# One 32-block arena per chain, and a fourth slot in the ring of feed-forward weights

## What is computed

```python
for i in range(DEPTH):                       # DEPTH = 2
    if i == 0:  mix = gla_mixer(h, ...)      # q,k,v,r and a low-rank gate; state S_t = diag(a_t) S_{t-1} + k_t v_t^T
    else:       mix = swa_mixer(h, ...)      # 16 query heads, 4 key/value heads, window 128, sinks
    h = layer_norm(ALPHA * h + mix, ln1_g[i], ln1_b[i])
    h = layer_norm(ALPHA * h + square(relu(h @ w_up[i])) @ w_down[i], ln2_g[i], ln2_b[i])   # 1024 -> 4096 -> 1024
    gate = sigmoid(h @ ple_w_gate[i] + ple_b_gate[i])
    h = h + gate * (p[i] @ ple_w_proj[i])
```

## Time and profile before

| what | value |
|---|---|
| runs | 3371.1 us median of 3 (3258.78 to 3663.18) |
| profiled execution | 3272.82 us |
| its slowest core (3), first to last instruction | 3271.2 us |
| the other cores | 3234.5 to 3269.6 us |
| mean granted TensorE clock of core 3 | 0.979 |
| TensorE busy | 3087.3 us, 94% |
| VectorE, ScalarE, GpSimd busy | 45%, 51%, 27% |
| DMA traffic | 584.44 MB, 179 GB/s |

### The profile page before, as it was taken

The page is one execution under the profiler, slowest core; times in us unless marked ns, Lnnn a source line. Parts: engine busy times, 40 slices in busy tenths (PEclk is TensorE's granted clock), DMA queues, the critical chain, the costliest instruction groups (busy, mean ns, idle before and its releaser), DMA issues.

```text
span 3271.2 us, 46722 instructions; the slowest of 8 cores (3234.5 to 3271.2 us)
## 1 busy us (share of the span) xinstructions
PE 3087.3 (94%) x15776; PEld 1447.5 (44%) x15776; DVE 1463.1 (45%) x2583; ACT 1665.6 (51%) x2939; POOL 878.7 (27%) x552
## 2 busy tenths in 40 slices
PE   6797998997999999999999999999999999999998
PEld 3343444443444444444444454444445444444443
DVE  2542324254353653545535255545525445454614
ACT  4662553653536445544654645545464645555452
POOL 1312213114133241413214123231412124141402
PEclk9898999999999999999999999999999999999999
DMA  8989789778896355474545644363553635344342
GB/s 196 236 201 218 221 211 189 210 186 190 257 186 214 142 189 196 155 223 147 190 157 180 206 150 150 135 199 117 201 177 141 229 132 180 128 147 168 142 165 83
DMA packets 88649, 584.44 MB, mean 179 GB/s; under 512 B 10112, under 2 KB 10368, under 8 KB 28160
## 3 DMA queue, kind: packets, MB, share of 16 engines
q1 hardware_dynamic: 78192, 513.09, 45.3%
q0 software_dynamic: 10224, 68.36, 14.3%
HBM read 592.62 MB, written 85.46 MB: 207 GB/s over the span
## 4 chain that ended last, share of the span: by engine, by line
PE 81%; DMA 10%; DVE 3%; issue 3%; ACT 2%; SPq 0%; POOL 0%; DVEq 0%; ACTq 0%; POOLq 0%
PE ps L704 31%; PE ps L1089 23%; PE ps L711 12%; PE ps L1124 6%; DMA mring<-wsb 4%; PE ps L1021 2%; DMA h<-x 2%; DMA mring<-ws 1%; DMA wsb<-mring 1%; PE ps L1132 1%; PE ps L740 1%; PE ps L1001 1%; PE ps L981 1%; DMA xT<-xs 1%; DMA sring<-wsb 1%
## 5 line engine op out<-in xcount | busy, mean ns | idle before, releaser
L1089 PE MATMUL ps<-mring,hid 128*128 128x512 bf16 x4096 | 937.5, 383 | 53.0 <-DMA mring<-wsb 30.2
L704 PE MATMUL ps<-xT,mring 128*128 128x512 bf16 x4096 | 927.8, 383 | 30.7 <-DMA mring<-wsb 14.6
L1089 PEld LDWEIGHTS ps<-mring,hid 128*128 128x128 bf16 x4096 | 394.3, 99 | 523.0 <-issue 92.9
L704 PEld LDWEIGHTS ps<-xT,mring 128*128 128x128 bf16 x4096 | 393.5, 99 | 518.0 <-issue 87.4
L758 POOL TENSOR_TENSOR h<-h,lnr_sb 128x1024 f32<-128x1024 f32 x128 | 304.8, 2385 | 795.9 <-ACT h L756 525.5
L711 PE MATMUL ps<-sring,xT 128*128 128x512 bf16 x2048 | 460.9, 381 | 5.3 <-DMA sring<-wsb 3.3
L1074 ACT ACTIVATE tmpa<-ps 128x512 f32<-128x512 f32 x512 | 304.6, 596 | 191.3 <-PE ps L704 188.9
L764 DVE SCALAR_TENSOR_TENSOR h<-h,ps 128x512 f32<-128x512 f32 x256 | 174.2, 682 | 424.2 <-PE ps L1089 366.3
L711 PEld LDWEIGHTS ps<-sring,xT 128*128 128x128 bf16 x2048 | 199.0, 98 | 247.5 <-issue 19.3
L759 POOL TENSOR_TENSOR h<-h,lnr_sb 128x1024 f32<-128x1024 f32 x128 | 302.9, 2371 | 14.5 <-POOL h L758 0.4
L1075 ACT ACTIVATE hid<-tmpa 128x512 bf16<-128x512 f32 x452 | 284.5, 630 | 38.2 <-ACT tmpa L1074 1.1
(11 more groups left out here) (114 smaller groups left out, 2740.0 us busy)
## 6 DMA issues: line engine op xcount, KB each, us to landing
mring<-wsb SPq DMA_DIRECT2D x240, 1024.0 KB, 6.0
sring<-wsb SPq DMA_DIRECT2D x126, 1024.0 KB, 6.6
lnr_sb<-lnr SPq DMA_DIRECT2D x32, 1024.0 KB, 6.8
wsb<-ws POOLq DMA_DIRECT2D x23, 1024.0 KB, 14.1
h<-x SPq DMA_DIRECT2D x32, 512.0 KB, 6.8
mring<-ws POOLq DMA_DIRECT2D x16, 1024.0 KB, 19.3
wsb<-mring SPq DMA_DIRECT2D x16, 1024.0 KB, 16.1
y<-h SPq DMA_DIRECT2D x32, 512.0 KB, 4.3
```

The source lines that it names most:

```text
L704: ins = h.matmul(ps[b.i][:], lhsT=wt[:, (m * 8 + kc) * 128:(m * 8 + kc + 1) * 128], rhs=xT[c][:, kc, :], start=(kc == 0), stop=(kc == 7))
L1089: ins = h.matmul(ps[b.i][:], lhsT=hid[:, kk, t * 128:(t + 1) * 128], rhs=wt[:, kc * 512:(kc + 1) * 512], start=(kk == 0), stop=(kk == 31))
```

## The change

- `hid` and the shared `ar` go. Each chain gets an arena of 32 blocks (`ars[c]`), in which the mixer's data lie first and the squared activations of the same job's feed-forward afterwards. `ebl` (GLA's decays) exists once per chain.
- `xnb` goes. Normalised rows are put into blocks of the chain's own arena that hold nothing at that point (X_IN, X_LN1, X_LN2, X_OUT).
- The sum of squares in GLA (L914 before) writes its unused squares over the quarter of q that has been read, and waits that named whole blocks now name the quarter of the tile.
- The waits on `hid_read` go.
- The SBUF set free makes a fourth slot of `mring`. The rule for the first three loads still says `k < 3`.

No DMA, matmul, or other operation is added or taken away. The planner makes a new order for all engines.

```diff
-        hid = sb("hid", [128, 32, G], BF16)
-        mring = [sb(f"mring{i}", [128, UW], BF16) for i in range(3)]
+        mring = [sb(f"mring{i}", [128, UW], BF16) for i in range(4)]
-        NAR = 33
-        ar = sb("ar", [128, NAR * 512], BF16)
+        ars = [sb(f"ar{c}", [128, 32 * 512], BF16) for c in range(2)]
-        xnb = sb("xnb", [128, NT, D], BF16)
-        ebl = sb("ebl", [128, 4, NT], F32)
+        ebls = [sb(f"ebl{c}", [128, 4, NT], F32) for c in range(2)]
...
+        def arena(c):
+            ar = ars[c]
...
+            def an(i, n=1, q=range(4)):
+                return [f"ar{c}.{k}.{r}" for k in range(i, i + n) for r in q]
...
-        A_Q, A_K, A_V, A_G, A_KH, A_KHT, A_A, A_GKL, A_OG = 0, 4, 8, 16, 24, 26, 28, 30, 31
+        A_Q, A_K, A_V, A_G, A_KH, A_KHT, A_A, A_GKL, A_OG = 0, 4, 8, 16, 24, 26, 28, 30, 30
+        X_IN, X_LN1, X_LN2, X_OUT = 24, (A_V, 24), 0, 8
+
+        def xnb(c, base, t):
+            ar, blk, an = arena(c)
+            return blk(base + 2 * t, 2), an(base + 2 * t, 2)
...
-        hid_read = [-1] * 4
...
+        def ln_norm(c, t, base):
+            xa, xr = xnb(c, base, t)
...
-            yield either([("dve", fv, 1.6), ("act", fa, 1.24)], hn(c, t) + [f"mv{c}_{t}", f"rstd{c}_{t}", f"nmr{c}_{t}"], [f"xnb{t}"])
+            yield either([("dve", fv, 1.6), ("act", fa, 1.24)], hn(c, t) + [f"mv{c}_{t}", f"rstd{c}_{t}", f"nmr{c}_{t}"], xr)
...
-                yield mmul(b, an(A_Q, 8), 0.25, f)
+                yield mmul(b, an(A_Q, 8, [t]), 0.25, f)
...
-                    if m == 0 and u % 2 == 0:
-                        yield Until(lambda u=u: hid_read[u // 2] >= j - 1)
...
-                    yield either([("act", fs, 0.63), ("dve", fq, 0.69)], [f"tmpa{i}", b], [f"hid{mi}"], drop=[b])
+                    yield either([("act", fs, 0.63), ("dve", fq, 0.69)], [f"tmpa{i}", b], an(mi), drop=[b])
...
-                        o = O("pe", f, [wres] + [f"hid{uu * 8 + kc}" for kc in range(8)], [banks[t]], 1.73, fill=[banks[t]] if uu == 0 else (), after=ups if uu == 0 else ())
+                        o = O("pe", f, [wres] + an(uu * 8, 8, [t]), [banks[t]], 1.73, fill=[banks[t]] if uu == 0 else (), after=ups if uu == 0 else ())
...
-                    if half == 1:
-                        hid_read[uu] = j
```

More of the change, by code:

```diff
@@ L500, in build_nc, with blk @@
         rinv = sb("rinv", [128, 4], F32)
-        def blk(i, n=1):
-            return ar[:, i * 512:(i + n) * 512]
-        def an(i, n=1, q=range(4)):
-            return [f"ar{k}.{r}" for k in range(i, i + n) for r in q]
+        def arena(c):
+            ar = ars[c]
+            def blk(i, n=1):
+                return ar[:, i * 512:(i + n) * 512]
+            def an(i, n=1, q=range(4)):
+                return [f"ar{c}.{k}.{r}" for k in range(i, i + n) for r in q]
+            return ar, blk, an
         def hn(c, t, hs=(0, 1)):
@@ L647, in p_loader, with turn_tile @@
                 state["pT"] = j + 1
-        def turn_tile(c, t):
+        def turn_tile(c, t, base):
+            xa, xr = xnb(c, base, t)
+            yield copy_op(xa, lambda: h_tok[c][:, t, :], hn(c, t), xr, 1.6)
             b = Bank()
@@ L663, in load_x @@
                 for t in range(NT):
-                    yield copy_op(xnb[:, t, :], lambda t=t: h_tok[c][:, t, :], hn(c, t), [f"xnb{t}"], 1.6)
-                    yield from turn_tile(c, t)
+                    yield from turn_tile(c, t, X_IN)
             elif g < straight:
@@ L736, in ln_transpose, with f @@
                 for t in range(NT):
-                    def f(h, t=t, bb=bb, half=half):
+                    xa, xr = xnb(c, base, t)
+                    def f(h, t=t, bb=bb, half=half, xa=xa):
                         for i in range(4):
                             kc = half * 4 + i
-                            ins = h.transpose(psb[bb[i // 2].i][:, (i % 2) * 512 + t * 128:(i % 2) * 512 + (t + 1) * 128], xnb[:, t, kc * 128:(kc + 1) * 128], identb[:])
+                            ins = h.transpose(psb[bb[i // 2].i][:, (i % 2) * 512 + t * 128:(i % 2) * 512 + (t + 1) * 128], xa[:, kc * 128:(kc + 1) * 128], identb[:])
                         return ins
-                    yield O("pe", f, [f"xnb{t}", "identb"], bb, 0.22, fill=bb if t == 0 else ())
+                    yield O("pe", f, xr + ["identb"], bb, 0.22, fill=bb if t == 0 else ())
                 for i in range(4):
@@ L776, in wo_tile, with pre0 @@
             if t > 0:
-                yield from ln_norm(c, t - 1)
+                yield from ln_norm(c, t - 1, base)
         lnctr = [0]
-        def pre0(c, g):
+        def pre0(c, g, j):
+            ar, blk, an = arena(c)
+            qtT = [blk(hd) for hd in range(4)]
+            ktT = [blk(4 + hd) for hd in range(4)]
+            v_tok = lambda t, hd: ar[:, (A_V + t * 2) * 512 + hd * 256:(A_V + t * 2) * 512 + (hd + 1) * 256]
+            og = ar[:, A_OG * 512:(A_OG + 2) * 512]
+            gkl = ar[:, A_GKL * 512:(A_GKL + 1) * 512]
+            ebl, en_ = ebls[c], f"ebl{c}_"
             li = lnctr[0]
@@ L893, in f @@
                         return ins
-                    yield mmul(b, an(A_Q + half * 2, 2) + [f"{srn}{half * 2}", f"{srn}{half * 2 + 1}"] + an(A_A + pi) + an(A_V + 2 * t + half), 0.45, f, after=gates)
+                    yield mmul(b, an(A_Q + half * 2, 2, [t]) + [f"{srn}{half * 2}", f"{srn}{half * 2 + 1}"] + an(A_A + pi) + an(A_V + 2 * t + half), 0.45, f, after=gates)
                 for half in range(2):
@@ L1059, in mlp @@
             U = UNITS[layer]
+            ar, hid, an = arena(c)
             yield Until(lambda: state["up"] == j)
@@ L1088, in f @@
                                 kk = uu * 8 + kc
-                                ins = h.matmul(ps[b.i][:], lhsT=hid[:, kk, t * 128:(t + 1) * 128], rhs=wt[:, kc * 512:(kc + 1) * 512], start=(kk == 0), stop=(kk == 31))
+                                ins = h.matmul(ps[b.i][:], lhsT=hid(kk)[:, t * 128:(t + 1) * 128], rhs=wt[:, kc * 512:(kc + 1) * 512], start=(kk == 0), stop=(kk == 31))
                             return ins
-                        o = O("pe", f, [wres] + [f"hid{uu * 8 + kc}" for kc in range(8)], [banks[t]], 1.73, fill=[banks[t]] if uu == 0 else (), after=ups if uu == 0 else ())
+                        o = O("pe", f, [wres] + an(uu * 8, 8, [t]), [banks[t]], 1.73, fill=[banks[t]] if uu == 0 else (), after=ups if uu == 0 else ())
                         o.rank = MLP
@@ L1107, in post @@
             for t in range(NT):
-                yield from ln_norm(c, t)
-            yield from ln_transpose(c, SM_LNC + layer * 32 + 16)
+                yield from ln_norm(c, t, X_LN2)
+            yield from ln_transpose(c, SM_LNC + layer * 32 + 16, X_LN2)
             yield from ln_residual(c, li)
@@ L1141, in post @@
                 if layer == 0:
-                    yield copy_op(xnb[:, t, :], lambda t=t: h_tok[c][:, t, :], hn(c, t), [f"xnb{t}"], 1.4)
-                    yield from turn_tile(c, t)
+                    yield from turn_tile(c, t, X_OUT)
                 else:
@@ L1155, in chain_stream @@
                 yield from my_turn("pre", j)
-                yield from (pre0(c, g) if layer == 0 else pre1(c, g))
+                yield from (pre0(c, g, j) if layer == 0 else pre1(c, g, j))
                 state["turn"] += 1
```

52 lines of the change are left out of this document (24 added, 28 removed).

## The result

The four runs shown of the changed kernel have a median of 3464.6 us (3360.7 to 3784.2), those of the kernel before beside them 3314.9 us (3256.7 to 3663.2). The wide spread is that of runs in which the cores of a die had a lower granted clock; without these the ratio is 1.0335, with a 95% interval of 1.0251 to 1.0419. A kernel with the same instructions in the same order was timed once more among the experiments (hidgate) at 1.0291 (1.0228 to 1.0354). The profiled execution took 3360.7 us, beside 3272.8 us before.

The account below looks back on a forecast made before the run. TensorE was taken as the bound, with winnable idle time in the first 1200 us, where weights are cast. Terms: 3272.8 − 60 (fourth slot) + 8 (start) + 76 (new order) = 3297 us, range 3225 to 3370.

Parts of the forecast that it names:

- rival B: Down projections of jobs 1 to 3: DMA engines stay the bound, the order adds bare stretches; 3351 us, chance 0.28.
- the fourth slot, −60 us: Up and down projections, first 1200 us: loads start one unit earlier, shortening `mring` waits and the low clock behind them; 60 us saved.
- The bounds, 25 to 83: Fourth slot's saving: 25 us, half of the plain loads' 45 and little clock, up to 83 us, the weights' whole share.
- The new order, +76 us: Layer-norm drains, mixer of job 3, attention of job 4: filler matmuls missing, 34 + 23 + 19 us, bounds 40 to 110.
- 11.4: Each of three layer-norm drains (after job 0's down, before job 3's up, after job 4's attention): 11.4 us lost.
- 23 + 11.4: Mixer of job 3: 23 us TensorE idle without filler, plus 11.4 us for the drain ahead of its up projection.
- 19 + 11.4: Attention of job 4: 19 us TensorE idle without filler, plus 11.4 us for the layer-norm drain behind it.
- the lower bound: New order: 40 us, if drains overlap with the other chain's transposes and VectorE shares its work with GpSimd.
- The start, +8 us: Start of kernel: `sring` casts 4 to 6 go behind all four `ebl` copies, TensorE waits; 8 us, bounds 3 to 15.
- What costs nothing: Moved rows and squares, finer names, dropped `xnb`: no cost; jobs 6 to 15: idle time may move 5 us either way.
- The signs that I had named: First 1200 us: `mring` waits of 10 to 25 us if right, above 45 us for B; new GLA and mask waits.
- the 135 to 170: First 1200 us: TensorE's idle time was to stay at 135 to 170 us if the forecast was right.

Follow-up runs that it names:

- hidgate: The changed kernel with the rule of `hid_read` kept (an up projection waits for the earlier down projection's read of its `hid` quarter); 1.0291 to the kernel before.
- plan3: The changed kernel with four slots in memory, its loads timed by the planner as if there were three; 3270.9 and 3272.5 us, about 1.00 to the kernel before.
- the pair without casts: Changed kernel with layer 1's 23 casts cut to 64 of 4096 columns, in four-slot order (1.0024), and the three-slot kernel with the same cut (0.9837).
- four slots in both: Two four-slot kernels with layer 1's casts cut to 64 columns: one in the four-slot order, 1.0024, one planned as three, 0.9875.
- keeping the turn: The changed kernel with the cast into the fourth `mring` slot issued in its own turn behind `sring`'s loads (`k < 4`); 1.0313 to the kernel before.
- the kernel that was to show it: The changed kernel with four slots planned as three and layer 1's casts cut to 64 of 4096 columns; 0.9875 to the kernel before.

## Why the prediction was wrong

The forecast was 3272.8 − 60 + 8 + 76 = 3297 us, a ratio of 1.007; the measured one is 1.029 to 1.034. From the profiled execution's 3272.8 us and 1.031 that makes 3374 us, just above my range of 3225 to 3370 (the profiled execution itself, 3360.7 us, lies in it). It is beyond rival B (3351 us, 2.4% over), which I had given 0.28 and whose account, DMA engines full in the down projections and bare stretches on top, is the one that came.

**The step that failed is the fourth slot, −60 us.** It was worth 0: 65.7 us of `mring` waits before and after, 63.0 with four slots and the order of three. The sentence that carried it, "a wait shorter than 6.9 us then goes", takes it that a load begun a unit earlier lands a unit earlier. In plan3 it began 6.7 us earlier than with three slots and was on its way for 5.7 us longer. The bounds, 25 to 83, excluded nothing gained. I had the reason on paper, 78 us of DMA work in a down projection of 55, and set it aside for a mean over the first 1200 us (0.80). Bursts don't see a mean: the engines are full between 640 and 710 us and at 0.19 in the mixer of job 3. With the lower end in place of 60 the sum would have been 3332 us.

The rule of the Trainium skill ("Perfetto Trace Analysis", Optimization Strategy), that a gap coming back on the engine to be saturated can mean too few buffers, asks for what this change did; here the gaps came back at 65.7 us with one buffer more, so by these runs it was no sign of too few. The other rule of the Trainium skill ("Trainium Kernel Development and Optimization", Key Constraints), that DMAs issued from SyncE, ScalarE and GpSimd run on the same 16 DMA engines, agrees with the stretch from 640 to 710 us, where casts (69.4%) and plain transfers (30.0%) fill the sixteen together.

**A term was missing, +50 us.** In the new order the same casts cost 94 us in place of 45, and I had taken order and loads as separate terms. My reading is this: where feed-forward runs bare, it wants a unit each 6.9 us while casts hold the engines, and loads of 28 to 50 us come of that, also for `sring`, which hardly waited before. Where the mixer runs bare, the engines rest. Spreading the casts gave back 27 us of it, moving them by two loads, which restored the order, all of it.

**The new order, +76 us**, was right in kind, and its size somewhat high: 61 us by the pair without casts, 49 with four slots in both. By stretches (cost over full-clock matmuls, casts left out): behind job 0's down projection 10.1 for 11.4; the mixer of job 3 with the drain at its end 24.7 for 23 + 11.4; attention of job 4 with its drain 26.6 for 19 + 11.4. So the mixer of job 3 and its drain overlap in part, as the lower bound had allowed. The agreement is in part luck, since my terms left the clock out of the mixer and the attention: there TensorE sat idle for 57 − 40.8 = 16 us and 91 − 72.8 = 18 us, where I had 23 + 8.9 and 19 + 8.9, and the rest of the cost is the clock, at 0.84 and 0.89.

**The start, +8 us.** The mechanism came as described, and the wait was of that size:

```profile
54.48 0.19 POOL L817 COPY ebl<-fbuf 128x4 f32<-128x4 f32 x1 [1.46 <-ACT fbuf L816]
55.00 1.60 POOL L600 DMA_DIRECT2D sring<-ws  x3 [0.33 <-issue]
```

```profile
65.51 6.82 PE L713 MATMUL ps<-sring,xT 128*128 128x512 bf16 x18 [7.63 <-DMA sring<-ws]
```

Three casts go behind the last copy, and TensorE waits 7.6 us (7.9 on core 6). But keeping the turn gained nothing that could be seen, so the 8 us seem to belong to the fourth cast and not to its place. Its issue on this core was at 55.0 us, not after 57; it is the order behind all four copies that holds.

**What costs nothing** did cost nothing, and the arenas gave back 8 us. The part behind job 5 changed by 1 us of idle time, within the 5 forecast. The signs that I had named: `mring` waits "still above 45 us" means B, and that came, as did the waits on GLA in job 3 and on masks in job 4 (3.8 us on L935, 2.4 on L1021 at most). TensorE's idle time, 193 us, was above the 135 to 170.

The sum with what was measured: −8 (arenas) + 0 (slot) + 61 (order, start included) + 50 (casts in that order) = 103 us, ratio 1.031. That it comes out is no proof, since the 61 and the 50 are differences of the same four ratios and add up to it whatever they are. It only shares the loss out. Still open is how much the slot would be worth with few casts and an unchanged order: the kernel that was to show it lands its loads 4 us sooner, but its order differs at the end of job 0's mixer.

## What to carry to other kernels

Before a buffer is added against load waits, take the DMA share inside the burst, not over the stage: here loads and casts of one phase needed more engine time (78 us) than its matmuls lasted (55), and a slot more only made each load start sooner and take longer. Where a planner sets the order, a changed ring size changes the order too, so build the old order with the new size and the new order with the old traffic before believing either. Look for the stretches where the DMA engines rest, and move matmuls of the hungry phase into them; in this kernel that was worth more than depth (the shift of the casts by two loads undid the whole loss).

## What was not expected of the hardware

In the full stretch from 640 to 710 us casts took 0.694 × 70 / 6.09 = 8.0 us of all sixteen engines per MB, plain transfers 0.300 × 70 / 5.60 = 3.75; over the whole span it had been 6.8 and 2.9. Reckoned in the same way, two other full stretches of this core give 7.8 and 3.1 us (480 to 560 us) and 8.1 and 3.2 us (890 to 990 us). So a cast cost 15 to 19% more where both run at once, a plain transfer 7 to 29%. A plain load of 1 MB was on its way for up to 45.6 us in the first of these stretches and for 49.5 us in the last, against a median of 6.
